# Router on turned raw rows, expert sort behind the places, SiLUs inside the chunk chain: a two-layer hybrid encoder trunk in fp32

## The reference

```python
for i in range(2):
    ada = silu(c) @ ada_w[i] + ada_b[i]
    sh1, sc1, g1, sh2, sc2, g2 = split(ada, 6)
    h = rms_norm(x) * (1 + sc1) + sh1
    x = x + g1 * (gdn_mixer(h) if i == 0 else fox_mixer(h))
    h = rms_norm(x) * (1 + sc2) + sh2
    x = x + g2 * hier_moe(h)
return rms_norm(x, final_norm)
```

## Time and profile before

| | |
|---|---|
| time before | 1684.03 us, median of 3 runs (1678.89 to 1686.05) |
| the profiled execution's own time | 1681.09 us |
| its span | 1679.3 us |
| mean granted clock of PE | 0.913 of full speed |
| gated DeltaNet, heads | about 60 to 555 us |
| out projection, router and sort, layer 0 | about 555 to 655 us |
| experts, layer 0 | about 655 to 920 us |
| attention, heads | about 983 to 1279 us |
| out projection, router and sort, layer 1 | about 1279 to 1381 us |
| experts, layer 1, and the end | about 1381 to 1679 us |

### The profile page before, as it was taken

How to read it: one execution, slowest core, us unless ns; L and a number is a source line. 1 busy time by engine, 2 the same in 40 slices (tenths; PEclk the granted TensorE clock), 3 DMA queues, 4 the chain that set the end, 5 groups by cost and what they waited for, 6 DMA issues and landing times. The chain is left out here.

```text
span 1679.3 us, 25626 instructions
## 1 busy us (share of the span) xinstructions
PE 1408.2 (84%) x9229; PEld 945.8 (56%) x9229; DVE 690.2 (41%) x1432; ACT 478.1 (28%) x1081; POOL 403.1 (24%) x607
## 2 busy tenths in 40 slices
PE   4998998999998876798977379999999957989871
PEld 2866776767786354454443366666664634445440
DVE  3554554455554255511101625555644454211114
ACT  4323333244423120111111334555441201111113
POOL 3322022022112001343421043443320012334320
PEclk9899999999999977899989579999999868999996
DMA  8253453451104343899997503111136328999994
GB/s 359 99 192 144 162 189 126 152 201 51 51 9 205 125 163 154 348 412 415 396 420 302 210 21 119 64 63 62 63 126 264 123 92 333 382 421 392 419 389 166
DMA packets 50712, 351.88 MB, mean 210 GB/s; under 512 B 12168, under 2 KB 12640, under 8 KB 25008
## 3 DMA queue, kind: packets, MB, share of 16 engines
q1 hardware_dynamic: 39008, 333.57, 50.3%
q0 software_dynamic: 11520, 16.83, 2.8%
q10 hardware_dynamic: 80, 0.04, 0.0%
HBM read 344.00 MB, written 27.34 MB: 221 GB/s over the span
## 5 line engine op out<-in xcount | busy, mean ns | idle before, releaser
L1164 ACT COPY arena<-PS 128x128 f32<-128x128 f32 (+3 forms) x328 | 154.6, 486 | 519.9 <-PE PS L797 182.6
L941 PE MATMUL PS<-Wr,arena 128*64 128x256 f32 x1856 | 230.7, 405 | 43.5 <-DMA Wr<-in_moe_w_gate_up_dram 37.1
L714 PE MATMUL PS<-hHi,Whi 128*128 128x512 f32 x512 | 224.1, 438 | 8.3 <-POOL Wlo L2124 5.1
L941 PEld LDWEIGHTS PS<-Wr,arena 128*64 128x64 f32 x1856 | 144.9, 147 | 146.9 <-issue 84.3
L716 PE MATMUL PS<-hHi,Wlo 128*128 128x512 f32 x512 | 202.2, 395 | 0.0
L715 PE MATMUL PS<-hLo,Whi 128*128 128x512 f32 x512 | 201.7, 394 | 0.0
L1938 DVE TENSOR_TENSOR arena<-arena,PS 128x128 f32<-128x128 f32 x72 | 20.7, 288 | 357.2 <-ACT arena L1369 354.6
L2124 POOL TENSOR_TENSOR Wlo<-Wr,Whi 128x512 fp32r<-128x512 f32 (+1 forms) x80 | 105.5, 1335 | 220.5 <-ACT Whi L1164 219.7
L2179 POOL DMA_INDIRECT y_rows<-arena x72 | 73.6, 1023 | 314.2 <-ACT arena L1164 302.8
L714 PEld LDWEIGHTS PS<-hHi,Whi 128*128 128x128 f32 x512 | 97.6, 191 | 44.2 <-issue 29.1
L716 PEld LDWEIGHTS PS<-hHi,Wlo 128*128 128x128 f32 x512 | 96.9, 189 | 21.8
(11 more groups left out here) (335 smaller groups left out, 2205.7 us busy)
## 6 DMA issues: line engine op xcount, KB each, us to landing
Wr<-in_moe_w_gate_up_dram SPq DMA_DIRECT2D x66, 2048.0 KB, 14.2
Dr<-in_ada_w_dram SPq DMA_DIRECT2D x42, 1024.0 KB, 6.0
Dr<-in_moe_w_down_dram SPq DMA_DIRECT2D x34, 1024.0 KB, 17.1
hT<-in_moe_w_down_dram SPq DMA_DIRECT2D x32, 1024.0 KB
Wr<-in_gdn_w_dram SPq DMA_DIRECT2D x8, 2048.0 KB, 8.7
Wr<-in_fox_w_dram SPq DMA_DIRECT2D x8, 2048.0 KB, 7.7
arena<-y_rows SPq DMA_DIRECT2D x16, 512.0 KB, 6.9
X<-in_x_dram SPq DMA_DIRECT2D x2, 2048.0 KB, 10.3
```

Source lines behind the costliest of these rows:

```text
L714: mm(out_ap, a_hi, b_hi, start=(k == 0), stop=False)
L941: last = mm(out_bank[C * g:C * g + C, 0:DE], at, w[:, k, g * DE:g * DE + DE], start=(k == 0), stop=(k == KD - 1))
L1164: return nc.scalar.copy(dst, src)
```

## The change

Five edits. (1) A new tile `modq` takes rows 3 and 4 of the conditioning (shift and scale of the second norm) with one value per partition and piece, by two transposing DMAs a layer, ahead of `gateB` in SP's queue. Before the out projection PE multiplies the shift by the router's weights, DVE adds that to the router's bias and scales the router's weights by 1 + scale. (2) The router's transposes read X itself (`rows_turned`) instead of `hrow`; `route` multiplies the logits by `rstd` as it adds the bias. The order of PE, ACT and DVE in the out projection is rewritten for it. `h_tile` stays, for the experts' gathers. (3) `by_rows` is moved ahead of the first `slot_table`, `order` directly behind it, and `plan_of_rows`, `item_rows`, `place_in` each one step earlier. (4) `silus` is cut into four steps, one behind each chunk's `vnew`; the second table load stands behind `osq`. (5) `project` and `project_pair` wait for `Wlo` piece by piece.

```diff
@@ SP, sublayer_rows
+                for j in range(2):
+                    load(modq[:, layer, j, :], ada_row(layer * 6 + 3 + j)[0].rearrange("(k p) -> p k", p=P), modq_in, slow=True)
                 load(gateB[:], ada_row(layer * 6 + 2)[0].partition_broadcast(P), gate_in)
@@ PE, project (project_pair alike)
-                    if f == 0:
+                    if m == 0:
                         if isinstance(s, int) and s < 2:
-                            pe.wait_ge(w_lo_pool, KD * (s + 1))
+                            pe.wait_ge(w_lo_pool, KD * s + k + 1)
                         else:
-                            pe.wait_ge(w_lo, (s - 1) * KD)
+                            pe.wait_ge(w_lo, (s - 2) * KD + (k + 1))
@@ PE, out_projection
+                pe.wait_ge(modq_in, 32 * (layer + 1))
+                for k in range(KD):
+                    last = mm(PS[3][:, 0:NG + NE], modq[:, layer, 0, k:k + 1].to_broadcast([P, P]), routW[:, layer, k, :],
+                              start=(k == 0), stop=(k == KD - 1))
+                last.then_inc(slots_ps, 1)
                 pe.wait_ge(ready, ready_n)
...
-                        if u >= NT + 2:
-                            norm_transposes(2 * layer + 1, u - NT - 2)
-                for n in range(2):
-                    narrow(2 * layer + 1, [n], routW[:, layer], NG + NE)
-                    norm_transposes(2 * layer + 1, n + 2)
+                        if u > NT:
+                            rows_turned(layer, u - NT - 1)
+                        if u == NT + 2:
+                            narrow(2 * layer + 1, [0], routW[:, layer], NG + NE)
+                narrow(2 * layer + 1, [1], routW[:, layer], NG + NE)
+                rows_turned(layer, NT - 1)
                 narrow(2 * layer + 1, [2, 3], routW[:, layer], NG + NE).then_inc(r_ps, 1)
+            def rows_turned(layer, n):
+                phase = 2 * layer + 1
+                pe.wait_ge(wo_ok, layer * WO + NT + n + 1)
+                if n >= 2:
+                    hT_ready(phase, n - 2)
+                for k in range(KD):
+                    last = tr(PS[2 + 2 * (n % 2) + k // 4][:, (k % 4) * P:(k % 4) * P + P], X[:, n, k * P:k * P + P], ident[:])
+                last.then_inc(n_tr, 1)
@@ ACT, norm: the last tile's take_tile(phase, 2) now stands ahead of its rstd_tile
@@ ACT, delta and silus
                     nc.scalar.mul(vnew[:, n % 2, :], PS[5][:, 0:P], rb[:, n:n + 1]).then_inc(vn_ok, 1)
+                    silus(s, gate_s[par], n)
                 act.wait_ge(o_ps, d + 1)
                 A(osq, PS[7][:], ACT.Square).then_inc(osq_ok, 1)
+                log_exp_tables()
...
+            def silus(s, gate, n):
+                if n == 0 and s is not None:
                     act.wait_ge(conv_ok, s * 3 + 2)
                     A(qkv[1], qkv[1], ACT.Silu)
+                if n == 1 and s is not None:
                     A(qkv[0], qkv[0], ACT.Silu).then_inc(sq_ok, 1)
+                if n == 2 and gate is not None:
                     A(gate, gate, ACT.Silu)
+                if n == 3 and s is not None:
                     act.wait_ge(conv_ok, s * 3 + 3)
                     A(qkv[2], qkv[2], ACT.Silu).then_inc(sq_ok, 1)
-                log_exp_tables()
@@ DVE, out_projection
+                dve.wait_ge(modq_in, 32 * (layer + 1))
+                link(TS(modq[:, layer, 1, :], modq[:, layer, 1, :], 1.0, None, ALU.add))
+                dve.wait_ge(slots_ps, 4 * layer + 1)
+                TT(routB[:, layer, :], routB[:, layer, :], PS[3][:, 0:NG + NE], ALU.add)
+                for k in range(KD):
+                    ins = TS(routW[:, layer, k, :], routW[:, layer, k, :], modq[:, layer, 1, k:k + 1], None, ALU.mult)
+                ins.then_inc(r_pos, 1)
...
                     if u > NT:
+                        take_tile(phase, u - NT - 1)
+                    if NT < u < 2 * NT - 1:
                         h_tile(phase, u - NT - 1)
-                    if u == 2 * NT - 1:
-                        take_tile(phase, 0)
-                take_tile(phase, 1)
+                    if u == 2 * NT - 2:
+                        h_tile(phase, 2)
+                take_tile(phase, NT - 1)
                 h_tile(phase, NT - 1)
-                for n in range(2, NT):
-                    take_tile(phase, n)
@@ DVE, route and experts
-                link(TT(lg, PS[6] ..., routB[:, i, :] ..., ALU.add))
+                for n in range(NT):
+                    ins = STT(out=lg[:, n, :], in0=PS[6][:, n * (NG + NE):(n + 1) * (NG + NE)], scalar=rstd[:, n:n + 1], in1=routB[:, i, :],
+                              op0=ALU.mult, op1=ALU.add)
...
                 place_slots(posf.rearrange("p k n -> p (k n)"))
-                slot_table(3 * i + 1, 0, FIRST)
                 by_rows(i)
+                slot_table(4 * i + 2, 0, FIRST)
+                order()
...
                 rows(0, 0)
+                plan_of_rows()
                 rows(1, 1)
-                order()
                 step(0, 0)
-                plan_of_rows()
+                item_rows()
                 step(1, 1)
-                item_rows(i)
+                place_in(FIRST, NI, 4 * i + 2)
                 step(2, 2)
```

More of the change, by code:

```diff
@@ L187, in build @@
         routW = sb("routW", [P, 2, KD, NG + NE])
+        modq = sb("modq", [P, 2, 2, KD])
         abW = sb("abW", [P, KD, 2 * H])
@@ L332, in build @@
         x_in = sem("x_in")
-        cols_ps, cols_ok = sem("cols_ps"), sem("cols_ok")
+        cols_ps = sem("cols_ps")
+        cols_ok = cols_ps
+        modq_in = sem("modq_in")
         act_setup = sem("act_setup")
@@ L406, in _, with load @@
             pairs = [0, 0]
-            def load(dst, src, s):
-                sp.dma_start(dst, src).then_inc(s, 16)
+            def load(dst, src, s, slow=False):
+                sp.dma_start(dst, src, allow_slow_non_contiguous=slow).then_inc(s, 16)
             def ada_load(item, q, slot):
@@ L669, in narrow @@
                     hT_ready(phase, n)
+                    if phase % 2 and n == 0:
+                        pe.wait_ge(r_pos, 4 * (phase // 2) + 1)
                     for k in range(KD):
@@ L921, in slot_products @@
                 def slot_products(part, c0, c1, cols_of):
-                    pe.wait_ge(r_pos, 3 * i + part)
+                    pe.wait_ge(r_pos, 4 * i + 1 + part)
                     for u in range(2 * NT):
@@ L1075, in project_pair @@
                     m, k = f // KD, f % KD
-                    if f == 0:
-                        pe.wait_ge(w_lo_pool, p * KD + 3 * KD)
+                    if m == 0:
+                        pe.wait_ge(w_lo_pool, p * KD + (2 * KD + k + 1))
                     if m == 0 and isinstance(p, int) and p == 0:
@@ L1211, in norm @@
                     act.wait_ge(wo_ok, (phase - 1) // 2 * WO + (NT if phase % 2 else 2 * NT) + n + 1)
+                    if phase % 2 and n == NT - 1:
+                        take_tile(phase, n - 1)
                     rstd_tile(phase, n)
-                    if 0 < n and phase < 4:
+                    if 0 < n and phase < 4 and not (phase % 2 and n == NT - 1):
                         take_tile(phase, n - 1)
@@ L1262, in take_product, with delta @@
                 cp(cin[m % 2][:, CONV - 1:], PS[m % 2][:]).then_inc(ev_pj, 1)
-            def delta(d, take, par, w_n=None):
+            def delta(d, s, take, par, w_n=None):
                 act.wait_ge(k_ps, d + 1)
@@ L1342, in _ @@
                     weights_hi(1, range(KD))
-            silus(0, None)
+            for n in range(NT):
+                silus(0, None, n)
+            log_exp_tables()
             step(1, 1, 2)
@@ L1351, in _ @@
             step(7, 1)
-            delta(7, lambda m: None, 1)
-            silus(None, gate_s[1])
+            delta(7, None, lambda m: None, 1)
             head_norm(7)
@@ L1548, in h_tile @@
                 if n >= 2:
-                    dve.wait_ge(n_tr, 4 * phase + n - 1)
                     if phase % 2:
                         dve.wait_ge(hr_out[n % 2], 16 * (2 * (phase // 2) + n // 2))
+                    else:
+                        dve.wait_ge(n_tr, 4 * phase + n - 1)
                 link(STT(out=hrow[n % 2], in0=X[:, n, :], scalar=rstd[:, n:n + 1], in1=scaleB[:], op0=ALU.mult, op1=ALU.mult))
@@ L1760, in route @@
                 dve.wait_ge(r_ps, i + 1)
-                link(TT(lg, PS[6][:, 0:NT * (NG + NE)].rearrange("p (n c) -> p n c", n=NT),
-                        routB[:, i, :].unsqueeze(1).to_broadcast([P, NT, NG + NE]), ALU.add))
+                for n in range(NT):
+                    ins = STT(out=lg[:, n, :], in0=PS[6][:, n * (NG + NE):(n + 1) * (NG + NE)], scalar=rstd[:, n:n + 1], in1=routB[:, i, :],
+                              op0=ALU.mult, op1=ALU.add)
+                link(ins)
                 grp, exp_l = lg[:, :, 0:NG], lg[:, :, NG:]
@@ L1850, in plan_of_rows, with blocks_of @@
                 link(red(plan_p.rearrange("p u a -> p (u a)"), look, AX_X, ALU.add))
```

(10 more changed lines are left out.)

23 lines of the change are left out of this document (9 added, 14 removed).

## The result

The changed kernel takes 1632.7 us (median of 4 runs, 1629.4 to 1635.6) against 1684.5 before; the ratio is 0.970, with a 95% interval of 0.967 to 0.972. The prediction was 1635 with a range of 1621 to 1654. The profiled execution took 1630.5 (span 1628.7) against the 1632.5 that the sum gave.

The account below looks back on a forecast made before the run. Bounds: PE in the DeltaNet layer, a serial chain from out projection to experts, then expert weight loads. Terms 17.3 + 4.9 - 1.0 + 2 x 8.9 + 2 x 4.8 = 48.6 off 1681.1, plus 2.9 for the median: 1635, range 1621 to 1654.

Parts of the forecast that it names:

- SiLUs: DeltaNet heads: table load and SiLU fit ACT's 2.00 hole between chunks, PE's waits at head changes shrink; 17.3 us gained.
- Rival F: DeltaNet heads: moving the SiLUs does nothing, as ACT is delayed elsewhere; 17 us less gain, 1652; chance 0.04.
- C: DeltaNet heads: PE stays slow where it was and fast heads meet other waits; the 14.6 halves, 1642; chance 0.10.
- Rival B: DeltaNet heads: ACT's table switch also costs a drain, second vnew 1.3 late; 7 us less gain, 1642; chance 0.08.
- Pieces of Wlo: Attention layer: PE's waits for POOL's Wlo go, 4.9 us gained; added waits cost nothing, at the other end 4.
- New loads and products: Before layer 1's out projection: modq loads hide, PE's products and DVE's small instructions cost 1.0 us, bounds 0 and 3.4.
- Rival D: Layer 1's out projection waits for dear element loads; 1695 at 0.5 us per packet; chance 0.03, slower.
- Router: From X to the routing: shorter chain, last tile assumed at half clock; 8.9 us a layer gained, bounds 4.5 to 10.6.
- rival E: Router at full clock and expert weight stream moving by 6: more gain than forecast, 1629; chance 0.08.
- rival A: Router and sort give little: clock falls at 604, second gather paces the loads; 13.4 us less gain, 1649; chance 0.16.
- Sort: Experts: fifth expert's load starts 5.5 earlier and moves the weight stream, first gather 0.6 late; 4.8 us a layer gained.
- The sum: Whole kernel: all terms together gain 48.6 us, profiled execution 1632.5, median 1635; chance of this forecast 0.48.

Follow-up runs that it names:

- hold_fifth: Changed kernel with the load of the fifth expert's gate and up weights held until gate_up of item 1 instead of item 0; 1631.0 us.
- silus_only: Kernel before with only the SiLUs cut into steps inside the chunk chain; 1665.0 us, ratio 0.989.
- sort_only: Kernel before with only by_rows and order moved and the planning steps made earlier; 1676.3 us, ratio 0.994.

## Why the prediction came out right, by its steps

**SiLUs (forecast 17.3).** Right in mechanism, a little low: 18.0 at the first eviction in the profile (15.8 up to the last `osq`, where I had 14.6) and 20 in the run of this edit alone (interval 13 to 25). The hole of 2.00 took the load and the SiLU, with 0.06 to spare where I had counted on 0.09: `vnew` keeps its spacing of 2.38 and 2.5. Rival F is out, and so is C. Rival B is out by one row: `osq` starts at 329.36 and takes 0.60, and the load begins at 329.97. The drain of about 1380 ns that the Trainium skill (ScalarE: Activation LUTs, section What ACT_TABLE_LOAD costs) puts beside the load shows nowhere in this trace: the engine goes from `osq` to the load and from the load to the SiLU within 0.02. The load itself is 1.28, as it says.

**Pieces of Wlo (forecast 4.9, other end 0.9).** Right in its stretch, 6.0, and wrong for the whole: edit 5 alone has a ratio of 0.999, and the kernel without it is as fast as the one with it. The term is mis-sized: 4.9 was booked and nothing arrived (1631.5 without the edit, 1632.7 and 1632.0 with it). The waits that were added, for which I wrote "so I take nothing", may take it back; the other end of that bound, 4 for 98 waits, would fit. With edits 4 and 5 the first eviction lies at 531.9 to 540.7 (mean 537.6 of eight), with edit 4 and without edit 5 at 534.0 and 533.1. Two profiles against eight with this scatter don't show it, so where the 5 us go stays open.

**New loads and products (forecast 1.0).** Right: the first eviction of layer 1 comes 3.3 behind the end of PE's last product of the heads, where it came 2.2 behind, so 1.1. `modq` lands about 2 before PE arrives. The 1.5 that I took for both loads is near too: for about one microsecond the DMA engines are 0.89 busy at 22 GB/s.

```profile
1238.00:1239.00 1.00, 1.00 (x4) 0.39 (x3) 0.68 (x3) 0.51 (x2) 0.00 (x0) 1.00 0.89 22
1239.00:1240.00 1.00, 1.00 (x9) 0.84 (x8) 0.97 (x3) 0.20 (x1) 0.00 (x0) 1.00 0.09 9
```

The estimate of 1.3 by the Trainium skill (DMA: Bandwidth & Descriptors, section Measured) agrees with these rows. Rival D was right that such loads can delay the layer, but not that two of them do: it takes eight to cost the attention layer 4 to 5.

**Router (forecast 8.9 a layer, bounds 4.5 to 10.6).** Mis-sized: from the first eviction to the routing it is 11.3 and 12.0 less, 10.9 and 11.6 to the end of the additions with `rstd`, which my 8.9 took in; both are above my upper bound. The 2.7 by which X comes later is 2.4 and 2.7. Behind X, the sum without a slow clock was 5.7 (from 605.4 to 611.1), and 5.6 was measured. The step that failed is "I assume that the last tile runs at half clock": it doesn't, as PE has no hole there any more, and the clock falls only later, in the sort (0.76 from 592 to 598, in which PE is busy for 0.64, then 0.50). That is 1.7 a layer. A further 1.0 in layer 1 is the chain before, which took 20.3 there and not the 19.3 of layer 0 from which I had worked. The four additions with `rstd` cost 0.4, I had 0.3. This is the router's half of rival E; rival A's is out.

**Sort (forecast 4.8 a layer).** The size was right, 9.1 in the run of its own, by luck, as the mechanism was not. I had the stream of weights moved by the start of its first load. `hold_fifth` shows that this start can be 5 later at no cost. What the layer waits for is the gather of item 4, and that hangs on POOL's order: it is issued behind the scatter of item 1. It came earlier as item 1 and the second table did, since the planning left DVE's path to the items: from the first `gate_up` to the issue of that gather it takes 24.7 to 25.6 with the new sort and 30.5 to 31.3 without, but for layer 0 of the kernel before and of `silus_only`, which have 27.6 and 27.5 (why isn't shown). So layer 1 gained 4.9 from the routing to the turn of item 4 (62.9 to 64.2 without, mean 63.6; 58.7 in `sort_only`), and layer 0 next to nothing beside that one profile and 3.1 beside the mean of the four without edit 3. I had written that the gather "lands with the end of the backlog" and so "moves by nearly the same" as the stream; it does not land there, and it is the cause.

The first gather is 1.8 later against the routing, where I had 0.6: 0.4 is the router's additions, some 0.5 the table behind `by_rows`, and 0.8 the copy of 1.05.

**The sum.** Single runs give 20.4, 20.6 (router less `modq`), 9.1 and -0.7, against 17.3, 16.8, 9.6 and 4.9. That 1635 was right to 2 us is in part luck: the router and the SiLUs gave 7 more and edit 5 gave 5.6 less. A version beats both kernels: the changed one with the gather of item 4 ahead of the scatter of item 1, 1620.3.

## What to carry to other kernels

Ahead of a stretch that is bound by transfers, ask which single arrival the engines wait for, and not when the transfers start: here the weights could start 5 us later for nothing, while one small gather a layer, issued ahead of a scatter in its queue, gave 12 us (9 of them seen in the stretches). Look at an engine's own queue for what stands in front of the transfer on which all others wait. And a chain with holes of known length is a place to put other work, if the longest piece of it fits the hole by its measured time.

## What the runs showed of the hardware that was not expected

Element loads hold up their issuing queue. SP in layer 1 of the changed kernel:

```profile
1218.10 14.51 SPq L411 DMA_DIRECT2D modq<-ada_rows  x2
1232.65 6.94 SPq L411 DMA_DIRECT2D gateB<-ada_rows  x1
1239.64 0.43 SPq L411 DMA_DIRECT2D shiftB<-ada_rows  x1
```

The two loads of 4 KB, behind the weights that were still under way, kept SP for 14.5 us (the first was issued in 0.5, the second took the rest) and the next one for 6.9; before, `gateB` was issued in 0.53. Layer 0 has 14.3 and 7.5. `gateB` landed some 3 ahead of its use all the same, but `shiftB` was issued 21.5 us behind `modq`, and a load that was wanted at once would have waited as long. With eight such loads SP stood for 24.9, and `gateB` then took 0.58.

A copy of 128 values on GpSimd that begins while a large TENSOR_TENSOR of DVE runs between SBUF tiles ends only with it. In layer 0 of the changed kernel the operation runs from 610.29 to 611.51 and the copy from 610.51 to 611.56; the same copy in layer 1 takes 1.05 too. A copy that begins later in such an operation takes less, and beside a DVE copy out of PSUM it takes its usual 0.2:

```profile
1326.46 0.96 DVE L1886 TENSOR_TENSOR arena<-arena,plan 128x768 f32<-128x768 f32 x1
1326.90 0.56 POOL L2244 COPY arena<-arena 128x1 int32<-128x1 int32 x1
```

```profile
666.86 0.68 DVE L1973 COPY arena<-PS 128x512 f32<-128x512 f32 x1
667.03 0.20 POOL L2227 COPY arena<-arena 128x1 int32 x1
```

PE could turn the rows of item 4 7.2 to 9.2 us behind the issue of their gather when weights were queued in the DMA engines, and those of item 0 after 3.0 when hardly anything was (issued at 612.54, turned at 615.54; DMA share 0.13). How much is still queued didn't set it in layer 0: it is 8.7 in the changed kernel and in `hold_fifth`, where some 5 us of weights more were still to move.
